# Two-layer diffusion backbone: the attention bias fetched ahead of the last modulation blocks, those blocks moved into later waits, the expert weight queue held for the first gather, and two more waits rearranged

## What is computed

```python
for l in range(2):
    sh1, sc1, g1, sh2, sc2, g2 = split(cond @ w_mod[l] + b_mod[l], 6)   # and the same for the context's conditioning
    u = rms_norm(h, norm1_g[l]) * (1 + sc1) + sh1
    y = token_mixers(u, ...)      # projection, 4 head groups, among them neighbourhood attention with a bias table
                                  # and differential attention with a headwise rms_norm of its own (the sub-norm)
    h = h + g1 * (y @ w_out[l])
    u = rms_norm(h, norm2_g[l]) * (1 + sc2) + sh2
    h = h + g2 * expert_choice_ffn(u, ...)   # 16 experts; each takes its top 2N/16 tokens, SwiGLU, scatter-add back
return rms_norm(h, final_g)
```

## Time and profile before

| what | value |
|---|---|
| three runs | 2165.78, 2160.51, 2165.67 us, median 2165.67 |
| the profiled execution | 2170.84 us; its span, first to last instruction, 2169.0 us |
| PE busy | 1967.1 us, 91% of the span |
| PEld, DVE, ACT, POOL busy | 57%, 32%, 24%, 16% |
| granted TensorE clock | 0.969 of full speed, mean |
| moved by DMA | 525.45 MB, mean 242 GB/s |

### The profile page before, as it was taken

How to read it: one execution, slowest core, us unless ns; L and a number is a source line. 1 busy time by engine, 2 the same in 40 slices (tenths; PEclk the granted TensorE clock), 3 DMA queues, 4 the chain that set the end, 5 groups by cost and what they waited for, 6 DMA issues and landing times.

```text
span 2169.0 us, 40965 instructions
## 1 busy us (share of the span) xinstructions
PE 1967.1 (91%) x18300; PEld 1229.6 (57%) x18300; DVE 699.4 (32%) x1324; ACT 518.2 (24%) x1122; POOL 341.7 (16%) x194
## 2 busy tenths in 40 slices
PE   6999979989969999999999899989895899998896
PEld 4656647755536555665555556557642666655553
DVE  3084467853430000000001525367725011111113
ACT  3001226650221111211121311236612111110112
POOL 0000037850000110011100005037800000000000
PEclk9999989999979999999999999989998899999999
DMA  9431140043398999999998211110035799999994
GB/s 398 174 129 39 39 189 1 2 144 144 139 374 342 388 392 394 390 395 382 387 359 327 102 61 73 39 40 2 1 155 198 323 427 426 427 426 427 427 426 180
DMA packets 43739, 525.45 MB, mean 242 GB/s; under 512 B 5232, under 2 KB 5232, under 8 KB 13488
## 3 DMA queue, kind: packets, MB, share of 16 engines
q1 hardware_dynamic: 35136, 492.19, 55.5%
q0 software_dynamic: 6992, 25.43, 3.7%
q10 hardware_dynamic: 1440, 5.24, 0.6%
HBM read 506.85 MB, written 15.99 MB: 241 GB/s over the span
## 4 chain that ended last, share of the span: by engine, by line
PE 70%; DMA 11%; DVE 7%; issue 4%; ACT 3%; PEld 3%; POOL 2%; ACTq 0%; SPq 0%; DVEq 0%; PEldq 0%; POOLq 0%
PE ps L845 14%; PE ps L553 11%; PE ps L839 9%; PE ps L851 7%; PE ps L738 6%; PE ps L673 4%; PE ps L571 4%; DMA ring<-in_w_exp 3%; PE ps L707 3%; PE ps L957 2%; PE ps L691 2%; POOL arena L1675 2%; DMA u<-in_w_exp 2%; PE ps L493 2%; DMA arena<-in_w_exp 2%
## 5 line engine op out<-in xcount | busy, mean ns | idle before, releaser
L553 PE MATMUL ps<-u,ring 128*128 128x512 f32 (+1 forms) x800 | 276.9, 507 | 0.0
L1675 POOL TENSOR_SCALAR arena<-arena,rsum 128x768 f32<-128x768 f32 (+1 forms) x120 | 232.0, 1949 | 182.3 <-DVE rsum L1485 142.0
L553 PEld LDWEIGHTS ps<-u,ring 128*128 128x128 f32 x800 | 151.7, 190 | 123.7 <-issue 115.6
L1602 DVE SCALAR_TENSOR_TENSOR arena<-arena,ps 128x512 f32<-128x512 f32 x40 | 27.4, 685 | 555.8 <-ACT arena L1176 555.8
L845 PE MATMUL ps<-ring,arena 128*32 128x256 f32 x3072 | 171.3, 379 | 0.7 <-ACT arena L1184 0.6
L839 PE MATMUL ps<-ring,arena 128*64 128x256 f32 x1408 | 160.2, 384 | 12.7 <-DMA ring<-in_w_exp 6.3
L1102 ACT ACTIVATE arena<-arena,negmax 128x768 f32<-128x768 f32 (+1 forms) x160 | 135.0, 844 | 127.9 <-DVE arena L1465 101.7
L839 PE MATMUL ps<-arena 128*64 128x256 f32 x1344 | 150.6, 380 | 13.3 <-DMA arena<-in_w_exp 9.6
L673 PE MATMUL ps<-arena 64*128 64x256 f32 (+3 forms) x576 | 120.0, 532 | 31.4 <-DVE arena L1465 21.5
L738 PE MATMUL ps<-u,ring 128*128 128x512 f32 (+1 forms) x384 | 141.2, 530 | 6.6 <-DVE u L1501 6.6
L845 PE MATMUL ps<-arena 128*32 128x256 f32 x2432 | 141.3, 388 | 5.5 <-ACT arena L1158 5.5
(11 more groups left out here) (197 smaller groups left out, 2343.1 us busy)
## 6 DMA issues: line engine op xcount, KB each, us to landing
ring<-in_w_exp SPq DMA_DIRECT2D x92, 2048.0 KB, 16.7
arena<-in_w_exp SPq DMA_DIRECT2D x80, 2048.0 KB, 17.3
ring<-in_w_mod SPq DMA_DIRECT2D x22, 2048.0 KB, 11.6
u<-in_w_exp SPq DMA_DIRECT2D x20, 2048.0 KB, 17.9
ring<-in_w_in SPq DMA_DIRECT2D x10, 2048.0 KB, 11.7
ring<-in_w_out SPq DMA_DIRECT2D x4, 2048.0 KB, 8.4
u_rows<-arena ACTq DMA_DIRECT2D x10, 512.0 KB, 2.9
arena<-in_w_mod SPq DMA_DIRECT2D x2, 2048.0 KB, 18.1
```

Of the source, the lines that this page charges most:

```text
L553: mm = pe.matmul(ps[:, bb, 0:n], w[:, k, P * ct:P * ct + P], u[:, k, t0:t0 + n], start=k == 0, stop=k == KD - 1)
L1675: pool.tensor_scalar(e0, e0, rsum[:, c0:c0 + 1], None, ALU.mult).then_inc(s["p_norm"], 1)
```

## The change

1. The bias is fetched ahead of block 8 instead of behind block 11. `SLOTS` follows.
2. Blocks 8 to 12 are done in the attention steps of the context tokens (five blocks, 2.5 steps apart, where there were four, 3 apart); 13 and 14 follow the second norm's sum; 15 to 20 are `MOD_R`; 21 to 23 (`MOD_G`) are done on PE between the index transposes and the first gather's arrival. `make_gain(0, 1)` moves behind the output projection.
3. SP waits for layer 0's first gather (`e_g` at 32) before it issues the third expert block, and the expert blocks take the slots in another order.
4. Two output tiles, not one, run over input tiles 0 to 5 ahead of the wait for the sub-norm, in both layers.
5. In layer 1 the second half of the next pair's gather is turned ahead of the pair's last down product, and the scatter's first four tiles wait only for the first half of the pair's output.

```diff
-        STREAM += [("mod", m) for m in range(8, MOD_BLOCKS)]
-
-        STREAM += [("bias", 0)] + [("mod", MOD_C + m) for m in range(4)]
-        STREAM += [("out", 0, 0), ("out", 0, 1)] + [("mod", m) for m in range(MOD_C + 4, 2 * MOD_BLOCKS)]
+        STREAM += [("bias", 0)] + [("mod", m) for m in range(8, 13)]
+        STREAM += [("out", 0, 0), ("out", 0, 1)] + [("mod", m) for m in range(13, 2 * MOD_BLOCKS)]
...
-        EXP_SLOTS = ((4, 5, 3, 0, 6, 7, 2, 1) * 10 + (4, 5, 3, 0, 6, 2, 1) * 2 + (4, 5), (0, 4, 5, 2, 3, 1, 8, 6, 7))
-        SLOTS = [[0, 1, 2, 3] * 4 + [0, 1] + [2, 3, 0, 2, 3, 0, 2, 1, 4, 5, 3, 0, 2, 1], [0, 2, 3, 1, 0, 2, 3, 1]]
+        EXP_SLOTS = ((2, 3, 6, 7, 1, 4, 5, 0) * 10 + (2, 3, 6, 1, 4, 5, 0) * 2 + (2, 3), (0, 4, 5, 2, 3, 1, 8, 6, 7))
+        SLOTS = [[0, 1, 2, 3] * 3 + [0, 1, 2, 3, 0, 2, 3, 0, 2, 3, 1, 4, 5, 0, 2, 3, 1, 4, 5, 0], [0, 2, 3, 1, 0, 2, 3, 1]]
...
-        MOD_N, MOD_R = range(MOD_C + 4, MOD_C + 6), range(MOD_C + 6, 2 * MOD_BLOCKS)
+        MOD_N, MOD_R, MOD_G = range(13, 15), range(15, 21), range(21, 2 * MOD_BLOCKS)
...
-        MOD_LATE = range(MOD_C, MOD_C + 4)
+        MOD_LATE = range(8, 13)
...
+                    if l == 0 and j == 2:
+
+                        sp.wait_ge(sig["e_g", 0], 32)
...
-                if l == 0:
-                    modulation(range(8, MOD_BLOCKS))
                 pe.wait_ge(sig["rp_add", l], since("rp_add", l) + 7)
                 if l == 0:
-                    pe.wait_ge(sig["mod_ev"], MOD_BLOCKS)
+                    pe.wait_ge(sig["mod_ev"], MOD_LATE[0])
...
-                    steps += [(32.3 + 3 * x, "mod", x) for x in range(4)] + [(33.3 + 3 * x, "pick", x) for x in range(4)]
+                    steps += [(32.3 + 2.5 * x, "mod", x) for x in range(5)] + [(33.3 + 2.5 * x, "pick", x) for x in range(5)]
...
+                    if i == 0:
+                        out_products(0, range(6))
+                        out_products(1, range(6))
+                        pe.wait_ge(sig["dn_done", l], since("dn_done", l) + 2)
                     if i >= 2:
                         pe.wait_ge(sig["o_ev", l], since("o_ev", l) + i - 1)
-                    for k in range(KD):
-                        if i == 0 and k == 6:
-
-                            pe.wait_ge(sig["dn_done", l], since("dn_done", l) + 2)
-                        for t0, n, c in wp:
-                            mm = pe.matmul(ps[:, 4 + 2 * (i % 2) + c, 0:n], w[:, k, P * ct:P * ct + P],
-                                           u[:, k, t0:t0 + n], start=k == 0, stop=k == KD - 1)
+                    mm = out_products(i, range(6 if i < 2 else 0, KD))
...
                 pe.wait_ge(sig["ut_ev", l], since("ut_ev", l) + 2 * nt)
-                pe.wait_ge(sig["mod_ev"], 2 * MOD_BLOCKS)
+                if both:
+
+                    for m in MOD_G:
+                        mod_products(m, 6 + m % 2)
+                        if m > MOD_G[0]:
+                            mod_pick(m - 1, 4, MOD_TOK["out"][(m - 1) % 2], 8 * (m - 1 - MOD_G[0]))
+                    pay()
+                    mod_pick(MOD_G[-1], 4, MOD_TOK["out"][MOD_G[-1] % 2], 8 * (MOD_G[-1] - MOD_G[0]))
+                pe.wait_ge(sig["mod_cp"], 2 * MOD_BLOCKS)
...
+                                if dn == 3 and pair + 1 < PAIRS and not both:
+                                    gather(1 - buf, pair + 1, range(2, 4))
...
-                        if pair + 1 < PAIRS:
+                        if pair + 1 < PAIRS and both:
                             gather(1 - buf, pair + 1, range(2, 4))
...
-                        pe.wait_ge(sig["e_y", l], pp * (2 * DN) + DN * half_p + DN)
+                        pe.wait_ge(sig["e_y", l], DN * pair + DN // 2)
                         pe.wait_ge(sig["e_xev", l], min(pair + 2, PAIRS) * 4)
                         for dt in range(KD):
+                            if dt == KD // 2:
+                                pe.wait_ge(sig["e_y", l], DN * pair + DN)
...
-                if l == 0:
-                    modulation(range(8, MOD_BLOCKS))
-                    dve.wait_ge(sig["mod_ev"], MOD_BLOCKS)
-                    make_gain(0, 1)
...
                 dve.wait_ge(sig["o_ev", l], since("o_ev", l) + 8)
+                if l == 0:
+                    dve.wait_ge(sig["mod_ev"], MOD_N[0])
+                    make_gain(0, 1)
                 norm("n2", l, parts_of(l, True))
```

More of the change, by code:

```diff
@@ L710, in _ @@
                     elif what == "mod":
-                        mod_products(MOD_C + i, 2)
+                        mod_products(MOD_LATE[i], 2)
                     elif what == "pick":
-                        mod_pick(MOD_C + i, 2, MOD_TOK["context"][i % 2])
+                        mod_pick(MOD_LATE[i], 2, MOD_TOK["context"][i % 2])
                 pay()
@@ L718, in _ @@
                 if l == 0:
-                    pe.wait_ge(sig["mod_ev"], MOD_C + 4)
+                    pe.wait_ge(sig["mod_ev"], MOD_N[0])
                 for i in range(2):
@@ L726, in _, with out_products @@
                 pe.wait_ge(sig["c_y", l], since("c_y", l) + 1)
+                def out_products(i, ks):
+                    for k in ks:
+                        for t0, n, c in wp:
+                            mm = pe.matmul(ps[:, 4 + 2 * (i % 2) + c, 0:n], w[:, k, P * (i % 4):P * (i % 4) + P],
+                                           u[:, k, t0:t0 + n], start=k == 0, stop=k == KD - 1)
+                    return mm
                 for i in range(KD):
@@ L872, in _ @@
                 pe.wait_ge(sig["r_slot", l], since("r_slot", l) + 1)
+                pe.wait_ge(sig["mod_ev"], 2 * MOD_BLOCKS)
                 for pp in range(PAIRS // 2):
@@ L1147, in _ @@
                 if both:
-                    for m in MOD_R:
+                    for m in (*MOD_R, *MOD_G):
                         act.wait_ge(sig["mod_pk"], m - 1)
@@ L1232, in _ @@
                             take_y(0, i)
+                        if more and not both:
+                            take_gather(1 - half_p, pp * 2 + half_p + 1, range(2, 4))
                         for i in range(NI):
                             take_y(1, i)
-                        if more:
+                        if more and both:
                             take_gather(1 - half_p, pp * 2 + half_p + 1, range(2, 4))
@@ L1439, in _ @@
                 if l == 0:
-                    steps += [(33.6 + 3 * x, "mod", x) for x in range(4)] + [(34.6 + 3 * x, "pick", x) for x in range(4)]
+                    steps += [(33.6 + 2.5 * x, "mod", x) for x in range(5)] + [(34.6 + 2.5 * x, "pick", x) for x in range(5)]
                 for _, what, i in sorted(steps, key=lambda x: x[0]):
@@ L1492, in _ @@
                     elif what == "mod":
-                        mod_copy(MOD_C + i, 2, MOD_TOK["context"][i % 2])
+                        mod_copy(MOD_LATE[i], 2, MOD_TOK["context"][i % 2])
                     elif what == "pick":
-                        mod_add(MOD_C + i, 2, 1, i)
+                        mod_add(MOD_LATE[i], 2, MOD_LATE[i] // MOD_BLOCKS, MOD_LATE[i] % MOD_BLOCKS)
                 wc = TOK if l == 0 else LAT
@@ L1587, in _ @@
                 if l == 0:
+                    dve.wait_ge(sig["mod_pk"], 2 * MOD_BLOCKS)
+                    for m in MOD_G:
+                        mod_add(m, 4, 1, m - MOD_BLOCKS, 8 * (m - MOD_G[0]))
                     dve.wait_ge(sig["mod_ev"], 2 * MOD_BLOCKS)
```

## The result

| | before | after |
|---|---|---|
| four runs, us | 2165.78, 2160.51, 2165.67, 2173.89 | 2141.97, 2146.89, 2144.55, 2141.13 |
| median | 2165.73 | **2143.26** |
| the profiled execution, its span | 2170.84, 2169.0 | 2141.97, 2140.2 |
| granted TensorE clock, mean | 0.969 | 0.972 |
| PE busy | 1967.1 us, 91% | 1964.8 us, 92% |

The ratio is 0.9892, with a 95% interval of 0.9866 to 0.9918: faster by 1.08%, or 23 us of the median before. The forecast was -26.0 and 2139.7 us. The two profiled executions differ by more than the medians, 28.8 us of span. Part of that difference turned out to be a finding, and the third set of experiments is about it.

A forecast was written before the change was run, and what follows sets the result against it. TensorE was taken as the bound through layer 0's experts, DMA in layer 1's. Terms -14.3 + 2.7 - 3.1 - 6.6 + 0 - 3.8 - 0.9 = -26.0 us, from 2165.67 to 2139.7 us; range 2130 to 2150.

The forecast's parts named there:

- the forecast's own: Whole kernel: all terms as summed, 2139.7 us within some 5 us; chance 0.67.
- Term 1: Start of layer 0's attention: four modulation blocks and VectorE's 7.72 us gain leave the path, -14.3 us.
- Term 2: Context steps of attention: five modulation blocks instead of four, +2.7 us, bounds 0 and 4.5.
- Terms 3 and 4: Sub-norm waits covered by a second output tile: layer 0 -3.1 us; layer 1 -6.6 us, including 3.1 of low clock.
- There is no clock to win: Layer 0's sub-norm: 232 instructions behind the wait ran at the first 24's pace, 0.32 against 0.33 us each.
- Term 5: Layer 0's first gather: three modulation blocks fit in PE's 17.43 us wait and the hold gains nothing, 0 us.
- Rival A: Layer 0's first gather: fewer blocks behind it let it run free, another -9 us, 2131; chance 0.12.
- Term 6: Read-back at layer 0's end: layer 1's first block is fetched later, so PE's wait goes, -3.8 us.
- Term 7: Layer 1's scatter: the last pair saves its copy's wait, -0.9 us, bounds 0 and 1.
- Rivals B and D: Layer 0's expert weights lag: B, paid once, 2152, chance 0.07; D, waits in seven later pairs, 2195, chance 0.02.

The follow-up runs named there:

- the third set of experiments: Kernels run on one chip beside the kernel before (median 2166.30 us, 23 runs), forcing either order of VectorE's second gain and POOL's bias instruction, plus the changed kernel again.
- x_force: Kernel before, with layer 0's second gain made to wait until POOL has added the mask to the bias: 2172.65 us, ratio 1.0029.
- x_gain: Kernel before, with layer 0's second gain made after the output projection, the four modulation blocks staying ahead of attention: 2163.11 us, ratio 0.9993.
- x_free: Kernel before, with POOL's addition to the bias made to wait until VectorE has made the second gain: 2165.85 us, ratio 0.999.
- x_gainsub: Kernel before, with the second gain moved behind the output projection and both layers' sub-norm waits covered: 2153.54 us, ratio 0.9933.
- x_nohold: Changed kernel without the hold on SP's queue, expert blocks 2 to 8 fetched as their slots come free: 2143.08 us, ratio 0.9903.
- x_hold0: Changed kernel with the hold ahead of expert block 0 instead of block 2: 2136.45 us, ratio 0.9869.
- x_hold1: Changed kernel with the hold ahead of expert block 1 instead of block 2: 2135.59 us, ratio 0.9862.
- x_slot: Changed kernel with slots 0 and 1 exchanged in the last two turns of the expert order: 2152.67 us, ratio 0.9936.

## Why the prediction was right, and where not

The time lies 3.6 us above the forecast and inside the range, and the case that came true is the forecast's own. By its terms:

**Term 1, -14.3.** The trace gives 14.2 in this place. But the term was taken from one profiled execution, and the step that failed is "a gain over 16 columns, which takes 7.72 us because POOL's bias instruction runs in the same 7.73 us". True of that execution, it is not true of all, as x_force shows, and the median carries between nothing and some 5 us of it, as x_gain and x_free do. What the term is worth in every execution is the modulation blocks: from the end of the last rotation to the second score tile it is 12.8 us in x_gain (286.05 to 298.85) and 13.9 in x_free (286.10 to 299.98), and 4.5 in the changed kernel (284.55 to 289.09). So 8 to 9 of the 14.3, and this is the largest error of the sum. No run moves the blocks alone: this share, the largest of all, is read from the stage in the traces. The step from x_gainsub (ratio 0.9933) to the changed kernel (0.9892, 0.9887) leaves room for it beside the other terms, but does not measure it. The stall in the profile of before also goes with the two profiled executions being 28.8 us apart and the medians 22.5.

**Term 2, +2.7.** The stage is 1.3 us longer in the trace; over all profiles the new order averages 181.0 and the old 179.8. Its scatter of 4 us is wider than the term, so the size stays open within its bounds.

**Terms 3 and 4, -3.1 and -6.6.** Layer 1 measured 6.7, clock and all, against the profile of before, and 5.5 against those of x_gain and x_force. Layer 0 measured 5.0: 3.4 in kernels whose sums take 4.51 us as before (90.56 to 87.2), and 1.7 more where the sums take 2.82. The granted clock in the sums is 0.62 in the first case and 1.00 in the second. The second occurs in five of the nine profiles with the new sub-norm and in none of the four with the old. But the sums stand ahead of the wait that the change removes, so these 1.7 us may be chance; what makes the clock hold there isn't settled. "There is no clock to win" was wrong in another way too. In the earlier trace rows the clock stayed at 1.00 behind the wait, but behind the same wait of 2.91 us in x_free it fell, to 0.66 in the mean of 495 to 505, and that stage took 93.4 us; in x_gain it took 91.7. Averaged over all profiles, the stage takes 91.6 us with the old sub-norm and 86.4 with the new.

**Term 5, 0.** The number is right: x_nohold equals the changed kernel, the three blocks are done 8.6 us ahead of the rows, and no expert block of layer 0 is late. The reason failed in half, in the step "blocks queued behind the one in service cost the gather nothing". The engines do take turns packet by packet, but a turn is lost for every packet of the gather while anything is queued. With two blocks left the weight queue empties when the gather is all but done (6 of its 224 packets are left in 618 to 620), so holding the rest cannot help; with one or none it does. Rival A was real, but belongs to another place of the hold: x_hold0 lies 6.6 us below x_nohold, and x_hold1 as low by its ratio.

**Term 6, -3.8.** The wait is gone in every profile of the new order except x_slot, which brings it back at 7.5 us and costs some 10. The six old orders wait between 2.4 and 3.9 us here, 3.2 in the mean, so 3.8 was near the upper end. From layer 0's first expert product to this turning, the wait included, they average 539.3 us, and the four profiles of the new order that wait neither here nor for expert weights 536.7.

**Term 7, -0.9.** From layer 1's first expert product to the last scatter all old orders need 452.2 to 452.7 us, all new ones 451.2 to 451.7: 1.0 us.

Rivals B and D did not come: PE waited for no weights in layer 0's experts. Their stage differs by up to 4 us between profiles (535 to 539 us in all, waits for weights and rows taken off), with dips of the granted clock at other times in each. The changed kernel's two have 538.5 and 537.6, the profile of before 535.4; that is no more than this scatter.

With these sizes the sum is -8.8 + 1.3 - 5.0 - 6.7 - 3.8 - 1.0 = -24.0, and the two comparisons measured 22.5 and 24.3 us between medians, with intervals that reach from 18 to 29 us. The stall's mean, between nothing and 5 us, would come on top. The mechanisms of the forecast hold but for the steps named; that the number came out so near is in part luck, because an overpriced first term and underpriced sub-norms partly cancel.

## What to carry to other kernels

Before a stall of a profile goes into a sum, ask what decides that it happens: where two events lie closer together than executions differ, force either order and time both, or price the term at zero and at its full size. A small transfer that matters beside a stream of large ones is served fast only when the stream's queue is empty, so hold the stream early enough for it to run empty while the small one still has packets to move, and leave just the blocks whose transfer the consumer can hide: here holding back all expert blocks or all but one gave the same time. Whatever is fetched beside the last read-back delays it, so let that fetch depend on a slot that comes free late.

## What the runs showed that was not expected

- A DVE instruction of 0.17 us with two operands in SBUF took 7.72 us when POOL's instruction of 7.73 us had started 0.04 us before it, and POOL was not delayed. In x_free, where POOL must come second, it took 0.18. The maximum of x_gain, whose input is in PSUM, ran its normal 0.96 us in the middle of POOL's 7.75. The Trainium skill, "SBUF — State Buffer", section "SBUF: two separate sides", says that the port pair the two engines share is held for a whole instruction by whichever starts first, and that DVE needs it for an instruction with two inputs in SBUF. The trace agrees.
- In the taps it is the other way round: DVE's 60 instructions keep 57.72 us, and POOL's 7.73 become 26.70. POOL got nothing done until the last tap had ended, though many of the taps began after it: it ended 7.61 us behind that tap, and in layer 1 of the kernel before 7.62. "Whichever starts first" does not foretell that.
- Against a queue of 16 KB packets the gather's 4 KB packets got one turn in two, and with that a fifth of the engines' time.
- The kernel before spread over 20 us in 23 runs on one chip, the changed one over 5.8 in four and 5.0 in six. Why it is the steadier one isn't explained by these runs.
